# Tiles of h and mixed laid 2048 bytes plus a step apart, another step in each part of the kernel

## What is computed

```python
def first_block(x, ...):
    h = rmsnorm(x, norm1_w[l])
    proj = h @ w_in[l]
    u_pool, q, k, v, z, a, bt, xr, gr = jnp.split(proj, cuts, axis=-1)
    ...
    mixed = jnp.concatenate([y_pool, y_gdn, y_lru], axis=-1)
    x = x + mixed @ w_out[l]
    x = x + conv_ffn(rmsnorm(x, norm2_w[l]), ffn_up[l], ffn_conv_w[l], ffn_down[l])
    return rmsnorm(x, final_norm_w)

def _hybrid_layer(x, ...):
    h = _rmsnorm(x, g_pre)
    u = h @ w_in                       # queries, keys, values, gates of three branches
    ...
    branches = (o_a * jax.nn.silu(a_z), o_b * jax.nn.silu(b_z), o_c * jax.nn.silu(c_z))
    y = gates[:, :, 0] * (branches[0] @ w_branch[0])
    for n in range(1, N_BRANCH):
        y = y + gates[:, :, n] * (branches[n] @ w_branch[n])
    return y @ w_out
```

## Time and profile before

| | us |
|---|---|
| median of 3 runs | 3546.27 (3545.81 to 3552.08) |
| the profiled execution | 3550.71 |
| its span, first to last instruction | 3548.9 |
| TensorE busy | 3418.4 |
| VectorE busy | 2147.2 |
| ScalarE busy | 1845.6 |
| GpSimd busy | 181.9 |

### The profile page before, as it was taken

How to read it: one execution, slowest core, us unless ns; L and a number is a source line. 1 busy time by engine, 2 the same in 40 slices (tenths; PEclk the granted TensorE clock), 3 DMA queues, 4 the chain that set the end, 5 groups by cost and what they waited for, 6 DMA issues and landing times. The chain is left out here.

```text
span 3548.9 us, 73417 instructions
## 1 busy us (share of the span) xinstructions
PE 3418.4 (96%) x28014; PEld 3333.6 (94%) x28014; DVE 2147.2 (61%) x3494; ACT 1845.6 (52%) x2837; POOL 181.9 (5%) x208
## 2 busy tenths in 40 slices
PE   7889699999999999999999999999999999999999
PEld 7888699999999998899999999999899999999999
DVE  6666556655656665667655555655567755555554
ACT  4443645535544454655646764444555555674443
POOL 1000010000000014000000000000000000000000
PEclk9999899999999999999999999999999999999999
DMA  4223355555555554344355445454334345444554
GB/s 175 95 95 110 118 185 170 176 198 176 179 189 181 187 190 163 131 150 158 134 183 202 162 159 188 178 191 176 131 143 155 139 177 194 176 149 178 184 195 166
DMA packets 90611, 584.17 MB, mean 165 GB/s; under 512 B 10480, under 2 KB 11120, under 8 KB 28400
## 3 DMA queue, kind: packets, MB, share of 16 engines
q1 hardware_dynamic: 88992, 577.60, 46.0%
q0 software_dynamic: 1488, 4.72, 0.4%
HBM read 580.19 MB, written 2.10 MB: 164 GB/s over the span
## 5 line engine op out<-in xcount | busy, mean ns | idle before, releaser
L183 PE MATMUL bank<-h,w_hi 128*128 128x256 f32 x5808 | 1660.0, 286 | 50.6 <-DVE w_lo L164 40.0
L164 DVE TENSOR_TENSOR w_lo<-raw,w_hi 128x768 fp32r<-128x768 f32 (+5 forms) x1202 | 1348.7, 1132 | 517.1 <-ACT w_hi L159 513.7
L184 PE MATMUL bank<-h,w_hi 128*128 128x256 f32 x5808 | 1627.6, 280 | 0.0
L185 PE MATMUL bank<-h,w_lo 128*128 128x256 f32 x5808 | 1625.8, 280 | 0.0
L159 ACT ACTIVATE w_hi<-raw 128x768 fp32r<-128x768 f32 (+5 forms) x1202 | 1105.4, 968 | 247.5 <-PE bank L185 226.8
L183 PEld LDWEIGHTS bank<-h,w_hi 128*128 128x128 f32 x5808 | 1097.7, 189 | 71.3 <-issue 31.1
L184 PEld LDWEIGHTS bank<-h,w_hi 128*128 128x128 f32 x5808 | 1098.4, 189 | 2.8 <-issue 1.4
L185 PEld LDWEIGHTS bank<-h,w_lo 128*128 128x128 f32 x5808 | 1097.6, 189 | 0.0
L183 PE MATMUL bank<-mixed,w_hi 128*128 128x256 f32 x2400 | 675.5, 281 | 24.9 <-DVE mixed L986 15.4
L184 PE MATMUL bank<-mixed,w_hi 128*128 128x256 f32 x2400 | 672.8, 280 | 0.0
L185 PE MATMUL bank<-mixed,w_lo 128*128 128x256 f32 x2400 | 672.4, 280 | 0.0
(11 more groups left out here) (357 smaller groups left out, 2697.9 us busy)
## 6 DMA issues: line engine op xcount, KB each, us to landing
raw<-in_w SPq DMA_DIRECT2D x485, 1024.0 KB, 4.8
raw<-in_w_br SPq DMA_DIRECT2D x96, 512.0 KB, 4.2
raw<-in_w_uq SPq DMA_DIRECT2D x8, 768.0 KB, 4.3
raw<-in_w_ukv SPq DMA_DIRECT2D x8, 512.0 KB, 3.4
bias_t<-in_bias POOLq DMA_DIRECT2D x16, 192.0 KB, 3.1
x<-in_x SPq DMA_DIRECT2D x4, 512.0 KB, 8.5
raw<-in_w_kr SPq DMA_DIRECT2D x4, 512.0 KB, 3.4
out_x<-x SPq DMA_DIRECT2D x3, 512.0 KB, 7.4
```

Of the source, the lines that this page charges most:

```text
L164: dve.tensor_tensor(w_lo[:, b % 2, c], raw[:, b, c], w_hi[:, b % 2, c].bitcast(F32), ALU.subtract).then_inc(S["lo_done"], 1)
L183: pe.matmul(o, w_hi[:, b % 2, c], a_hi, start=start and k == t0, stop=False)
L184: pe.matmul(o, w_hi[:, b % 2, c], a_lo, start=False, stop=False)
L185: last = pe.matmul(o, w_lo[:, b % 2, c], a_hi, start=False, stop=stop and k == t0 + nt - 1)
```

## The change

`h` and `mixed` become rooms that are 128 and 384 elements longer. Four views of each are made, with a step of `gap` elements (4 bytes each) after each tile of 512 elements. View 0 is used in the mixers, 1 in the feed-forward part, 2 and 3 in the first and second layer. Every place that reads or writes h or mixed names the view of its part; here only one of each kind is shown. The instructions of all five engines and their order are the same. The rooms are 512 and 1536 bytes longer, so mixed begins 512 bytes later, and what follows it 2048 bytes later.

```diff
+H_GAPS = (1, 8, 4, 5)
+MIXED_GAPS = (9, 16, 2, 24)
...
-        h = sb("h", [KT, 2 * SEQ], F32R)
-        mixed = sb("mixed", [KT, 2 * SEQ], F32R)
+        h_room = sb("h", KT * 2 * SEQ + P, F32R)
+        mixed_room = sb("mixed", KT * 2 * SEQ + 3 * P, F32R)
+
+        def spread(room, gap):
+
+            return room[:, 0:KT * (2 * SEQ + gap)].rearrange("p (k s) -> p k s", k=KT)[:, :, 0:2 * SEQ]
+
+        h = [spread(h_room, gap) for gap in H_GAPS]
+        mixed = [spread(mixed_room, gap) for gap in MIXED_GAPS]
...
-            act.activation(h[:, tile(k), 0:SEQ], x[:, tile(k), :], ACT.Copy, scale=gain).then_inc(S["h_hi"], 1)
+            act.activation(h[ns][:, tile(k), 0:SEQ], x[:, tile(k), :], ACT.Copy, scale=gain).then_inc(S["h_hi"], 1)
...
-                        act.activation(mixed[:, bass.ds(2 * i + s, 1), 0:SEQ], fp[:, s, :].unsqueeze(1),
+                        act.activation(mixed[1][:, bass.ds(2 * i + s, 1), 0:SEQ], fp[:, s, :].unsqueeze(1),
...
-                a_hi, a_lo = of(h)(k)
+                a_hi, a_lo = of(h[0])(k)
...
-            way_out(B_WOUT, 0, 0)
+            way_out(B_WOUT, 0, 0, src=0)
...
-                        unit(pe, n, 2 * s, of(h), [(bank[0][:, 0:SEQ], 0, KT, True, True)], normed(pe, 1) if s == 0 else None)
+                        unit(pe, n, 2 * s, of(h[1]), [(bank[0][:, 0:SEQ], 0, KT, True, True)], normed(pe, 1) if s == 0 else None)
...
-                    unit(pe, n, b, of(h), [(bank[b % 2][:, 0:SEQ], 0, KT, True, True)])
+                    unit(pe, n, b, of(h[l + 2]), [(bank[b % 2][:, 0:SEQ], 0, KT, True, True)])
...
-                    unit(pe, n, b, of(mid, SLOT[br]), [(bank[1][:, 0:SEQ], 0, 8, True, True)])
+                    unit(pe, n, b, of(mid[l + 2], SLOT[br]), [(bank[1][:, 0:SEQ], 0, 8, True, True)])
```

More of the change, by code:

```diff
@@ L533, in mix @@
                 act.wait_ge(S["oz"], j + 1)
-                act.activation(mixed[:, bass.ds(MIX_GDN + j, 1), 0:SEQ], oy[:, :].unsqueeze(1), ACT.Copy).then_inc(S["mix_hi"], 1)
+                act.activation(mixed[0][:, bass.ds(MIX_GDN + j, 1), 0:SEQ], oy[:, :].unsqueeze(1), ACT.Copy).then_inc(S["mix_hi"], 1)
                 side(4)
@@ L588, in recur @@
                 act.wait_ge(S["lru_y"], i + 1)
-                act.activation(mixed[:, bass.ds(MIX_LRU + 2 * i, 2), 0:SEQ], lh[:, :, :], ACT.Copy).then_inc(S["mix_hi"], 1)
+                act.activation(mixed[0][:, bass.ds(MIX_LRU + 2 * i, 2), 0:SEQ], lh[:, :, :], ACT.Copy).then_inc(S["mix_hi"], 1)
             def blocks(i, mix):
@@ L613, in blocks @@
                             act.wait_ge(S["pool_y"], b + 1)
-                            act.activation(mixed[:, MIX_POOL + b, 0:SEQ], py[:, b, :], ACT.Copy).then_inc(S["mix_hi"], 1)
+                            act.activation(mixed[0][:, MIX_POOL + b, 0:SEQ], py[:, b, :], ACT.Copy).then_inc(S["mix_hi"], 1)
             act.wait_ge(S["pool_d"], 4)
@@ L985, in recur @@
                 two = bass.ds(MIX_LRU + 2 * i, 2)
-                dve.tensor_tensor(mixed[:, two, SEQ:2 * SEQ], lh[:, :, :], mixed[:, two, 0:SEQ].bitcast(F32),
+                dve.tensor_tensor(mixed[0][:, two, SEQ:2 * SEQ], lh[:, :, :], mixed[0][:, two, 0:SEQ].bitcast(F32),
                                   ALU.subtract).then_inc(S["mix_lo"], 1)
@@ L1192, in mix @@
                 fill(2)
-            unit(pe, 0, 0, of(h), [(bank[0][:, 0:SEQ], 0, KT, True, True)], normed(pe, 0))
+            unit(pe, 0, 0, of(h[0]), [(bank[0][:, 0:SEQ], 0, KT, True, True)], normed(pe, 0))
             pe.wait_ge(S["const_in"], 16)
@@ L1266, in _, with way_out @@
             pe.wait_ge(S["gr"], LB)
-            def way_out(n, i, added, third=None):
+            def way_out(n, i, added, third=None, src=1):
                 for b in range(4):
@@ L1273, in way_out @@
                         up_done(third, b)
-                    unit(pe, n, b, of(mixed), [(bank[b % 2][:, 0:SEQ], 0, KT, True, True)],
+                    unit(pe, n, b, of(mixed[src]), [(bank[b % 2][:, 0:SEQ], 0, KT, True, True)],
                          products(third) if third is not None and b == 0 else None)
-            way_out(B_WOUT, 0, 0)
+            way_out(B_WOUT, 0, 0, src=0)
             with pe.Fori(1, 4) as i:
-                way_out(B_WOUT + i, i, 0)
+                way_out(B_WOUT + i, i, 0, src=0)
             sum_squares(pe, 0)
@@ L1313, in down @@
                             up_done(third, b)
-                        unit(pe, n0 + 8 + i, b, of(mixed), [(bank[b % 2][:, 0:SEQ], 0, KT, True, True)],
+                        unit(pe, n0 + 8 + i, b, of(mixed[1]), [(bank[b % 2][:, 0:SEQ], 0, KT, True, True)],
                              products(third) if first and b == 0 else None)
@@ L1701, in head_tail @@
                 elif k == 3:
-                    out_hi(T, place(br, j))
+                    out_hi(l, T, place(br, j))
             def pair_body(l, i, hooks):
@@ L1938, in head_tail @@
                 elif k == 3:
-                    out_lo(T, place(br, j))
+                    out_lo(l, T, place(br, j))
             def pair_body(l, i, hooks):
@@ L2076, in _, with lat @@
         def _(pe):
[L2078 to L2080 removed]
+            def lat(l, first, n):
+                return lambda k: (mid[l + 2][:, LAT + first + k % n, 0:SEQ], mid[l + 2][:, LAT + first + k % n, SEQ:2 * SEQ])
             def free(n, b):
@@ L2212, in comb_body @@
                     if b % 2 == 0:
-                        unit(pe, n, b, of(h), [(bank[0][:, 0:SEQ], 0, KT, True, True)])
+                        unit(pe, n, b, of(h[l + 2]), [(bank[0][:, 0:SEQ], 0, KT, True, True)])
                         continue
@@ L2226, in _ @@
                     if b == 7:
-                        unit(pe, n, bb, of(h, 8), [(bank[0][:, 0:SEQ], 0, 8, False, True)])
+                        unit(pe, n, bb, of(h[l + 2], 8), [(bank[0][:, 0:SEQ], 0, 8, False, True)])
                     else:
@@ L2230, in _ @@
                         nt = 8 if b == 6 else KT
-                        unit(pe, n, bb, of(h), [(bank[bb % 2][:, 0:SEQ], 0, nt, True, b != 6)], normed(pe, l + 2) if b == 0 else None)
+                        unit(pe, n, bb, of(h[l + 2]), [(bank[bb % 2][:, 0:SEQ], 0, nt, True, b != 6)], normed(pe, l + 2) if b == 0 else None)
                 def latents(k):
```

58 lines of the change are left out of this document (28 added, 30 removed).

## The result

The changed kernel takes 3581.83 us (median of 4 runs, 3579.93 to 3582.94), the kernel before 3549.18 us over its four runs by then (3545.81 to 3558.47). The ratio is 1.0087, 95% interval 1.0074 to 1.0100: slower, by 0.9%, and clear of the 0.2% that a measurement can tell. It was forecast as faster, at 3532 us, and the time lies above the range, which ended at 3558 us.

A forecast was written before the change was run, and what follows sets the result against it. The prediction took TensorE's rate through 8704 three-matmul groups as the bound; its only term, 14.5 us off for reads, took the median 3546.3 us to 3531.8, forecast as 3532 us, range 3498 to 3558 us.

The forecast's parts named there:

- What bounds the kernel: TensorE, busy 96% of the span: 8704 groups of three matmuls at 350 ns, 3046 us or 86%.
- The reads: TensorE's reads of h and mixed: spread tiles save 3.3 ns in half of the 8704 groups, 14.5 us.
- the two rhythms: Distances between starts of groups in different stretches of the kernel before: 350 ns and 353.3 ns, 3.3 ns apart.
- The upper end: Worst case for the group's rhythm with the new placement: 3.8 ns more for all 8704 groups, +33 us.
- the 16 groups of the gates: First block, lines 1206 to 1208: weights 48 bytes apart instead of 512, uneven, 353.8 ns a group.
- The rival "slower": Starts off the 32-byte grid cost 5680 groups 3.8 ns each, 21 us, giving 3568 us; chance 0.17.
- The rival "no effect": The 10 ns beside the columns are weight change and matmul start, addresses don't matter: 3546 us; chance 0.30.
- the estimate of one more line: From the skill's 16-byte lines: a run of 256 elements starting inside a line touches 65 lines, not 64.
- The writes, the followers, the clock: ScalarE and VectorE writes of h and mixed, and tensors after mixed: nothing taken; granted clock and split durations stay.
- What is late next: TensorE's feeders, splits and transfers: a unit of 16 groups shorter by 27 ns changes none; the saving stays.
- The larger gain: Rival: the 10 ns are mostly colliding reads; spreading removes a fifth, 6 ns a group, 52 us: 3494 us; chance 0.05.
- The 10 ns beside the columns: Part of each 116.7 ns matmul beyond 106.7 ns for 256 columns; 30 ns a group, at most 261 us.

The follow-up runs named there:

- the run with 192 bytes everywhere: Changed kernel's text without steps, all tiles of h and mixed beginning 192 bytes past a multiple of 256 (kernel before: 32); 3522.53 us, ratio 0.9919.
- 112 bytes everywhere: Changed kernel's text without steps, all tiles of h and mixed beginning 112 bytes past a multiple of 256 (kernel before: 32); 3501.98 us, ratio 0.9865.

## Why the prediction was wrong

**What bounds the kernel: right.** TensorE's rhythm over 8704 groups is what the change moved, and 48.1 us of rhythm went with 32.2 us of span.

**The reads: the wrong step.** The prediction took "one step of the two rhythms, 3.3 ns, for half of the groups", since "some tiles meet a better place". It took for granted that the kernel before stands at a middling place. The runs show that it stands at one of the best six of the sixteen on the grid of 16 bytes: 112 is better, 192 mostly, 16 is its equal, 240 is 1 ns worse, and 144 was once 1 ns better and once 4 worse. Spreading the tiles trades that place for the mean of all, 353.5 ns on the grid of 16 bytes and more off it. The term of the sum was -14.5 us of rhythm; it measured +48.1 us, of which 32.2 reached the span.

**The bound that was too small.** The upper end was 33 us, from the 16 groups of the gates at 353.8 ns. The rhythm itself lost 48 us; that the span's 32.2 us lie under 33 is luck, since a third of the loss was given back. The row was right for what it was: their weights step by 48 bytes, and in 16 steps they visit all sixteen multiples of 16 once modulo 256, whose mean is 353.5. I read that row as a few unlucky groups, when by the table it was the forecast for any step of 16 bytes. It wasn't an upper bound for steps of 4, 8, 20 and 36 bytes, which leave that grid. After the change, the same 16 groups take, from the timeline of TensorE:

```profile
33.60 0.28 PE L1216 MATMUL m<-h,ab_hi 128*128 128x256 f32 x1
...
39.31 0.28 PE L205 MATMUL bank<-h,w_hi 128*128 128x256 f32 x1
```

5.71 / 16 = 356.9 ns, where they took 353.8.

**Two readings of the rows that were wrong.** The prediction said that the rhythm before is the same to 0.1 ns from tile to tile for 70 us. The earlier trace rows is a mean. In the starts to 1 ns, the groups of that same window take 347, 349, 351 and 353 ns in turn for most of it. And "340 to 360 ns" for the gates came from a timeline that prints 10 ns: the two groups meant take 350 and 357 ns, and all sixteen 347 to 360. So the unevenness that was held against "no effect" is of the size that the kernel has everywhere. That a stretch keeps its rhythm was right, as the run with 192 bytes everywhere shows.

**The rival "slower": right in sign, wrong in its mechanism.** It put the cost on a start off a grid of 32 bytes, for 5680 groups, and 3568 us. But the feed-forward part and mixed in the second layer, the 3024 groups on that grid, lost 4.0 to 6.6 ns as well, and its own 5680 groups lost 34.6 us, 6.1 ns each. So its price was too low and its extent too narrow. I gave it 0.17 because its row was one of 16 groups. The prediction named a pattern that comes back every 16 groups as the sign of a gain; it came back every 4 and 8, and was the sign of a loss.

**The rival "no effect", and the rule of the Trainium skill.** The page "SBUF — State Buffer", section "SBUF: two separate sides", gives TensorE a port of its own and a second one for loading weights, on which it waits for no other engine. By that the time would have stayed. As far as the other engines go, the trace agrees: the rhythm is the same with them at work and at rest. That TensorE's own reads don't disturb each other the runs contradict: w_lo alone moved by 80 bytes, and the activations kept at their place against w_hi, give 360 ns in place of 340, also where no other engine is at work. Its lines of 16 bytes fit, and the estimate of one more line was the right direction: no place off the grid of 16 was below 355 ns, and on the grid nine of sixteen are below 356.

**The writes, the followers, the clock: right.** The split of 1280 elements takes 1492 and 1259 ns as before, and the granted clock is 0.991 where it was 0.990.

**What is late next: wrong.** The prediction had "The saving stays on the path", and the wait for w_lo was to stay as it is. A third of the loss was taken up on the way to the span, and 41% of the gain with 112 bytes everywhere; the wait for w_lo went from 40.0 us to 37.0 and to 49.0. With this step alone set right, the forecast would still have been faster.

**The larger gain: there, but not from this change.** The 10 ns beside the columns are indeed not fixed. They are 6.6 ns (113.3 less 106.7) at the best places. But it is not spreading that gets at them; the right equal placement does.

## What to carry to other kernels

When TensorE runs back to back on short matmuls with new weights each time, measure the distance of starts to a tenth of a nanosecond, and try the distance between activations and weights modulo 256 bytes: eight parts of one kernel can test eight places in a single run. Test the best of them again in all parts, since a place can have two rhythms. Give all tiles the best place and keep it by steps that are multiples of 256 bytes; uneven steps give about the mean of the places that they visit. And ask of the present state whether it is already better than the mean before expecting anything from a change to "many" values.

## What the hardware showed that I had not expected

- The distance between starts of the same matmul (128 by 128 float32r weights, 256 columns, full clock) goes from 113.3 to 123 ns with nothing changed but where the tiles lie. With all at 112 bytes instead of 32 the kernel takes 1.3% less.
- The rule has a period of 256 bytes: a step of 256 leaves 350 ns, a step of 128 gives 353.3.
- Two rhythms can last at one place, 340.0 and 353.3 ns at 192 bytes, for tens of microseconds each. I don't know what chooses between them; 112 bytes kept to the low one nearly throughout, and with 192 everywhere a stretch that had settled never changed.
- The place of w_lo alone moved the time by 2.8%, from 3502 to 3601.5 us, in one run. The rhythm is 360 ns against 340 also where VectorE, ScalarE and GpSimd are at rest.
